# A norm turn after a seven-product matmul stage, taken by halves of the tokens

## What is computed

```python
        f = (jax.nn.gelu(gate, approximate=True) * val) @ w_down[l]     # 2816 -> 1024
        h = h + rms_norm(f, ln_ffn_post[l])
    ...
        h = rms_norm_2(x, norm1[l])                                     # second block, x is h above
        proj = h @ w_in[l]
```

## Time and profile before

| | |
|---|---|
| median of 3 runs | 2959.04 us (2957.28 to 2969.57) |
| the profiled execution | 2959.0 us, span 2957.2 us |
| TensorE matmul busy | 2835.6 us, 96% |
| VectorE, ACT, GpSimd busy | 62%, 43%, 21% |
| mean granted TensorE clock | 0.989 |

### The profile page before, as it was taken

How to read it: one execution, slowest core, us unless ns; L and a number is a source line. 1 busy time by engine, 2 the same in 40 slices (tenths; PEclk the granted TensorE clock), 3 DMA queues, 4 the chain that set the end, 5 groups by cost and what they waited for, 6 DMA issues and landing times.

```text
span 2957.2 us, 47458 instructions
## 1 busy us (share of the span) xinstructions
PE 2835.6 (96%) x19678; PEld 2274.4 (77%) x19678; DVE 1848.0 (62%) x2351; ACT 1269.7 (43%) x1879; POOL 623.0 (21%) x313
## 2 busy tenths in 40 slices
PE   8999998889899999999899999999899999999999
PEld 6877777777688888788678867766578888888887
DVE  3157778852599999866685554565645766653446
ACT  4145555542554555443543433343433423333334
POOL 4310122221100000254151200000012122245443
PEclk9999999999999999999999999999899999999999
DMA  6443330002423333465544553435544344465664
GB/s 216 151 121 114 110 131 30 27 26 79 143 89 106 102 101 107 155 220 180 175 133 153 164 178 122 129 112 160 192 150 131 115 150 145 150 216 196 211 238 171
DMA packets 306280, 413.79 MB, mean 140 GB/s; under 512 B 13569, under 2 KB 189834, under 8 KB 306066
## 3 DMA queue, kind: packets, MB, share of 16 engines
q1 hardware_dynamic: 291090, 363.56, 38.6%
q10 hardware_dynamic: 14976, 47.19, 4.2%
HBM read 280.64 MB, written 130.06 MB: 139 GB/s over the span
## 4 chain that ended last, share of the span: by engine, by line
PE 80%; DVE 8%; DMA 4%; issue 3%; ACT 3%; SPq 1%; POOL 1%; DVEq 0%; ACTq 0%; POOLq 0%
PE ps L511 17%; PE ps L2767 16%; PE ps L3300 13%; PE ps L3082 10%; PE ps L2124 5%; PE ps L695 4%; PE ps L1544 4%; PE ps L2175 2%; PE ps L2194 2%; DVE cb L3385 2%; PE ps L2152 1%; PE ps L1607 1%; PE ps L2155 1%; DMA kl<-qk_lo 1%; DMA residual<-src 1%
## 5 line engine op out<-in xcount | busy, mean ns | idle before, releaser
L477 POOL TENSOR_TENSOR wl<-wraw,wh 128x1024 fp32r<-128x1024 f32 x62 | 157.4, 2538 | 1103.0 <-ACT wh L472 1093.4
L511 PE MATMUL ps<-xh,wh 128*128 128x512 f32 x752 | 237.9, 398 | 5.2 <-POOL wl L477 2.3
L511 PE MATMUL ps<-xl,wh 128*128 128x512 f32 x752 | 233.3, 392 | 0.0
L511 PE MATMUL ps<-xh,wl 128*128 128x512 f32 x752 | 232.9, 391 | 0.0
L472 ACT ACTIVATE wh<-wraw 128x1024 fp32r<-128x1024 f32 x78 | 82.4, 1056 | 266.0 <-PE ps L511 205.3
L2756 POOL TENSOR_TENSOR h_dl<-h_dr,h_dh 128x1024 fp32r<-128x1024 f32 x36 | 94.7, 2633 | 477.8 <-ACT h_dh L2738 477.6
L511 PEld LDWEIGHTS ps<-xh,wh 128*128 128x128 f32 x752 | 139.6, 189 | 46.7 <-issue 9.0
L2767 PE MATMUL ps<-h_dh,h_fh 128*128 128x512 f32 x448 | 174.8, 390 | 0.7 <-POOL h_dl L2756 0.7
L2767 PE MATMUL ps<-h_dh,h_fl 128*128 128x512 f32 x448 | 174.4, 389 | 0.0
L2767 PE MATMUL ps<-h_dl,h_fh 128*128 128x512 f32 x448 | 174.3, 389 | 0.0
L511 PEld LDWEIGHTS ps<-xl,wh 128*128 128x128 f32 x752 | 142.4, 189 | 30.3
(11 more groups left out here) (507 smaller groups left out, 7634.6 us busy)
## 6 DMA issues: line engine op xcount, KB each, us to landing
h_fr<-act_d SPq DMA_DIRECT2D x60, 512.0 KB, 3.9
act_d<-act SPq DMA_DIRECT2D x16, 1792.0 KB, 6.7
wraw<-in_w_in SPq DMA_DIRECT2D x48, 512.0 KB, 5.0
h_dr<-in_w_down SPq DMA_DIRECT2D x44, 512.0 KB, 4.8
r_raw<-in_w_up SPq DMA_DIRECT2D x38, 512.0 KB, 3.9
residual<-src ACTq DMA_DIRECT2D x32, 512.0 KB, 5.1
w_raw<-in_w_up SPq DMA_DIRECT2D x32, 512.0 KB, 5.1
l_fr<-act_d SPq DMA_DIRECT2D x31, 512.0 KB, 3.9
```

The costliest lines, as they stand in the source:

```text
L477: nc.gpsimd.tensor_tensor(wl[:, s, :, :], wraw[:, s, :, :], wh[:, s, :, :].bitcast(F32), ALU.subtract).then_inc(w_lo, 1)
L511: mm = nc.tensor.matmul(ps[:, bank + h, :], w, x[:, h * HALF:(h + 1) * HALF], start=start and k == 0, stop=stop and k == 2)
```

## The change

The turn is made by halves of the tokens. The second half of `f` is complete after P7, so its norm, the new residual and `xh`, `xl` of the second half are made while P4 is multiplied; after P4 the first half follows, while TensorE multiplies the second half by the first two units. Sums of a half (`half_sums`) are made on four column strips of 128 tokens each; squares of the new second-half rows go to `sq1`, which is the memory of `xl`'s first halves. Residuals move in half tiles of 256 KB. Since `xh`'s and `xl`'s second halves are written during P4, P4's steps get homes elsewhere (`last`): three new ones, and a fourth in the first-half parts of `xh` for step 39, so that the loads of steps 36 to 38 wait only for a few sums. Between P4's steps ACT and VectorE take rows of the second half. Beside that, step 2's cast and low part are moved up by one tap pass.

The core of the diff:

```diff
+        def half_sums(of, start, stop, bank, to):
+            for j in range(4):
+                mm = nc.tensor.matmul(ps[QUARTERS[j], bank, to], ones[:, :], of[:, j * EIGHTH:(j + 1) * EIGHTH],
+                                      start=start, stop=stop)
...
+        def second_half_squares_act(act, m):
+            if m < 4:
+                act.wait_ge(down_added, down_added_by(down1, "P3", m))
+            else:
+                act.wait_ge(down_added, down_added_by(down1, "P7", m - 4))
...
+        def second_half_row_dve(dve, kt):
+            s = kt % 2
+            if kt == 0:
+                h1_pe.wait(dve, "spread", 0)
+            h1_dve.done(nc.vector.tensor_tensor(y[:, kt, SECOND], y[:, kt, SECOND], ps[:, 7, :], ALU.mult), f"m{kt}")
+            h1_dve.wait(dve, f"m{kt}", 0)
+            if kt >= 2:
+                h1_dve.wait(dve, f"l{kt - 2}", 0)
+                h1_act.wait(dve, f"s{kt - 2}", 0)
+            dve.wait_ge(h_loaded[s], 16 * (4 + kt // 2 + 1))
+            dve.wait_ge(src_stored[s], 16 * ((16 + kt) // 2))
+            h1_dve.done(nc.vector.scalar_tensor_tensor(
+                out=src[:, s, SECOND], in0=y[:, kt, SECOND], scalar=col("ln_ffn_post", kt), in1=hres[:, s, SECOND],
...
+        def second_half_act(act, kt):
+            tile = src[:, kt % 2, SECOND]
+            h1_dve.wait(act, f"r{kt}", 0)
+            h1_act.done(nc.scalar.activation(xh[:, kt, SECOND], tile, ACT.Identity, scale=col("norm1_2", kt)), f"x{kt}")
+            nc.scalar.activation(y[:, kt, SECOND], tile, ACT.Identity, scale=col("norm1_2", kt))
+            h1_act.done(nc.scalar.activation(sq1[:, kt, FIRST], tile, ACT.Square), f"s{kt}")
+            act.dma_start(residual[kt][:, SECOND], tile).then_inc(src_stored[kt % 2], 16)
...
         def down_load(sp, d, i):
-            if i >= 8 or (i >= 4 and not d.later):
+            if name == "P4" and d.last:
+                if c < 3:
+                    sp.wait_ge(loaded, down_loaded_by(d, i - 4))
+                    sp.wait_ge(down_done, down_done_by(d, d.steps.index(("P6", len(d.kts) - 1))))
+                    sp.wait_ge(g_sum, down_sums_by(d, d.steps.index(("P7", (0, 0, 4)[c]))))
+                else:
+                    sp.wait_ge(down_done, down_done_by(d, i - 4))
+            elif i >= 8 or (i >= 4 and not d.later):
                 sp.wait_ge(down_done, down_done_by(d, i - 4))
...
             for i in range(8, len(down1.steps)):
+                if i == LAST1 + 3:
+                    for kt in (0, 1):
+                        second_half_loads(sp, kt)
+                elif i == LAST1 + 5:
+                    second_half_loads(sp, 2)
                 down_load(sp, down1, i)
...
             ff1_tap(act, FF_TILES - 1, "g")
+            down_hi_act(act, down1, 2)
             ff1_tap(act, FF_TILES - 1, "v")
-            down_hi_act(act, down1, 2)
             ff1_gelu(act, FF_TILES - 1)
...
+            second_half_root_act(act)
+            down_hi_act(act, down1, LAST1 + 3)
+            for kt in (0, 1, 2):
+                second_half_act(act, kt)
+            down_hi_act(act, down1, LAST1 + 4)
+            for kt in (3, 4):
+                second_half_act(act, kt)
+            down_hi_act(act, down1, LAST1 + 5)
+            second_half_act(act, 5)
+            first_half_squares_act(act, 4)
...
-            post_sums_pe(pe, 24, KT - 2)
-            spread_pe(pe, 3)
-            paced_units(pe, U_FA, 0, 16, 32, 4)
+            second_half_products(pe, 0, 1, {
+                2: lambda pe: first_half_sums_pe(pe, 24), 3: lambda pe: second_half_square_sums(pe, range(0, 4)),
+                5: first_half_spread_pe, 7: lambda pe: second_half_square_sums(pe, range(4, KT))})
+            second_half_products(pe, 1, 3, {})
+            first_half_units(pe)
...
                 for x in "gv":
                     ff1_taps(dve, t, x)
-                    if not more and x == "v":
+                    if not more and x == "g":
                         down_lo_dve(dve, down1, 2)
```

More of the change, by code:

```diff
@@ L130 @@
     kept2: list
+    last: list
 CHUNK = 64
+EIGHTH = T // 8
 @dataclass
@@ L568, in spread_pe, with spread_half_pe @@
             mm.then_inc(spread_done, 1)
+        def spread_half_pe(of, half, row):
+            rows = ROWS[row]
+            for w, j in ((spread_even, 2 * row), (spread_odd, 2 * row + 1)):
+                mm = nc.tensor.matmul(ps[:, 6 + half, j * EIGHTH:(j + 1) * EIGHTH], w[rows, :], of[rows, :],
+                                      start=True, stop=True)
+            return mm
         def rstd_copy_act(act, k):
@@ new lines, in second_half_sum_dve, with second_half_sums_pe @@
+        def second_half_sum_dve(dve, m):
+            h1_act.wait(dve, f"q{m}", 0)
+            if m == 0:
+                dve.wait_ge(stat_root, 3)
+                ins = nc.vector.tensor_copy(ss[:, SECOND], sq[:, 0, SECOND])
+            else:
+                h1_dve.wait(dve, f"a{m - 1}", 0)
+                ins = nc.vector.tensor_tensor(ss[:, SECOND], ss[:, SECOND], sq[:, m % 2, SECOND], ALU.add)
+            h1_dve.done(ins, f"a{m}")
+        def second_half_sums_pe(pe):
+            pe.wait_ge(down_added, down_added_by(down1, "P3"))
+            h1_dve.wait(pe, f"a{KT - 1}", 0)
+            h1_pe.done(half_sums(ss[:, SECOND], True, True, STAT_BANK, FIRST_COLS), "sum")
@@ new lines, in second_half_root_act, with second_half_reciprocal_dve, second_half_spread_pe @@
+        def second_half_root_act(act):
+            h1_pe.wait(act, "sum", 0)
+            h1_act.done(nc.scalar.activation(root1[:, :], ps[:, STAT_BANK, FIRST_COLS], ACT.Sqrt,
+                                             bias=small[:, 0:1], scale=1.0 / D), "root")
+        def second_half_reciprocal_dve(dve):
+            h1_act.wait(dve, "root", 0)
+            h1_dve.done(nc.vector.reciprocal(root1[:, :], root1[:, :]), "rec")
+        def second_half_spread_pe(pe):
+            h1_dve.wait(pe, "rec", 0)
+            h1_pe.done(spread_half_pe(root1, 1, 0), "spread0")
+            h1_pe.wait(pe, "spread0", 0)
+            h1_pe.done(spread_half_pe(root1, 1, 1), "spread")
@@ new lines, in second_half_square_sums, with second_half_products @@
+        def second_half_square_sums(pe, kts):
+            for kt in kts:
+                h1_act.wait(pe, f"s{kt}", 0)
+                mm = half_sums(sq1[:, kt, FIRST], kt == 0, kt == KT - 1, STAT_BANK, SECOND_COLS)
+            h1_pe.done(mm, f"p{kts[-1]}")
+        def second_half_products(pe, u, bank, after):
+            for kt in range(KT):
+                h1_dve.wait(pe, f"l{kt}", 0)
+                if kt == 0:
+                    pe.wait_ge(w_lo, U_FA + u + 1)
+                    pe.wait_ge(evac_done, U_FA + u - 1)
+                    pe.wait_ge(down_added, down_added_by(down1, "P4", bank))
+                half_tile(bank, u, kt, SECOND)
+                if kt in after:
+                    after[kt](pe)
```

281 lines of the change are left out of this document (201 added, 80 removed).

## The result

Over 20 runs each the changed kernel took 2965.36 us (median; 2957.05 to 2970.67) and the kernel before 2957.66. The ratio is 1.0024 with a 95% interval of [1.0016, 1.0032]: about 7 us slower. That is under the 0.5% that I had called measurable for this kernel, but clear of zero: with 20 runs the interval is 0.1% to either side. The forecast was 4.5 us faster, and 2965.4 lies 1.4 us above its range. The profiled execution of the change took 2961.96 us (span 2960.2), 3.4 us under its median.

What follows compares the result with a forecast made beforehand. TensorE was taken as the bound, with VectorE pacing the norm turn. 2959.0 us less 2.4 (start of the down stage) less 2.1 (third unit's start, after the loss before the last products) gave 2954.5 us; range 2944 to 2964.

Steps and rivals of the forecast that it cites:

- part 4: First half, after the last products up to the third unit: that unit starts at 1486.2 against 1488.26, -2.1 us.
- part 1: Start of the down stage: one 5.28 us wait becomes 0.9 and 4.1 us; -2.4 us, ends 0 and -4.
- part 3: Second half beside the seventh product: TensorE waits 8.1 us before the last products, the clock falls; 11.8 us lost.
- lower end: Start of the down stage: if the 4.1 us wait costs the clock again, 2.8 is given back, gain 0.
- part 2: Loads of the seventh product's operand steps, the first three issued early: nobody waits for them, cost 0.
- Without the cold clock: Case for the start of the third unit if the clock stays up: -5.7 us in place of -2.1.
- third rival: Adds from row 2 on, both halves: the residual's round trip becomes the bound, 2964.6 us; chance 0.20.
- first rival: Half-width adds beside GpSimd's splits: engines do not take turns, wait 3.7 us, clock stays, 2946 us; chance 0.17.
- second rival: Before the last products: operands arrive in time, no wait, third unit -12.2 us, 2942.8 us; chance 0.08.
- deciding point: Residual's round trip in both halves: it decides once a half tile lands later than 3.3 us.

Runs made afterwards that it cites:

- e5: The changed kernel run again without any edit: ratio to the kernel before 1.0020 [1.0008, 1.0031].
- e3: The change, with casts and low parts of the seventh product's last two operand steps ahead of most second-half rows: ratio to before 1.0005.
- e2: The kernel before with only the change's start part (step 2's cast and low part ahead of the value half's taps): ratio to before 1.0003.
- e8: e7, with TensorE summing squares of the first half's first two rows between the second half's products: ratio to before 1.0020.
- e9: e7, with VectorE's copies out of the last product's banks one row later each, so row 5 comes first: ratio to before 0.9998.
- e10: e9, with TensorE summing squares of the first half's first two rows between the second half's products: ratio to before 0.9994.
- e7: e3, with VectorE's copies out of the last product's banks, and ACT's squares of them, ahead of rows 5 to 7: ratio to before 1.0016.
- e4: The change, with VectorE's T1 moved behind the eviction of fa: ratio to before 1.0024.
- e1: The change, with its start part (step 2's cast and low part moved up) put back as before: ratio to before 1.0019.
- e6: The change, with step 37's cast and low part ahead of half squares and sums, and P7's adds between the square sums: ratio to before 1.0030.
- e12: The kernel before run again without any edit: ratio to before 1.0007 [0.9997, 1.0017].
- e13: The change, with fa's bank copied out raw and multiplied with the reciprocal root later: ratio to before 1.0020.
- e16: The change, with the cast and low part of step 41, the last operand step, one row later: ratio to before 1.0037.

## Why the prediction was wrong

The sign was wrong: +6 to +7 us where I had -4.5. The loss that I took as the largest came as forecast. The gains that were to outweigh it came out too small: the first half and the way to the third unit (part 4) by 6.1 us, the start (part 1), as far as times can tell, by all of its 2.4.

**Cost, part 3, held.** From the first seventh product to the first of the last products I had 30.8 us (from 1413.35, where it begins before) and the traces 31.3 and 30.8; up to the end of the last product 11.0, measured 10.1. TensorE waited 7.0 us where I had 8.1, since it came 1.8 us later than I had it (1437.8 for 1436.0), by the start wait, and by sums and spreads in halves. The rows came within 1.1 us of the list: 1436.8 for the split of step 40 was 1437.8, step 41's 1444.1 was 1444.65. Some luck is in the sum: the last products began 0.7 us later than I had them, but only 8 matmuls there ran at the 1.2 GHz level (12 in e5), where I had 14, which more than made up for it. e3 shows that the wait costs about the time it seems to.

**Cost, part 4, failed, in two terms above all.** Up to the first half's spread I had 7.3 us, measured 7.8. "Then 0.7, eight rows of 2.1, the last low part, and 0.7 of waits for residuals: 19.1" took 21.3 (1462.64 to 1483.97): the third row's square waited 1.98 us for a buffer that TensorE frees only once it has gone through the second half's products. The third row's store left later by that, and the fifth row, which needs the same buffer, waited 0.98 us for it. And "unit 0 ends 1.1 later ... the third unit's weights are then cast and split" took 8.1 us where I had 4.7. I read in the earlier trace rows that the third unit waited for wl and took the split as the only thing there, at 2.5 us, where in the trace of before it took 3.87 beside T1. That trace already needed 7.3 us from the last low part to the unit, so 4.7 was too little before any change. The chain from the last row over squares, root, reciprocal (1.75), spread, copy (1.03) and eviction (1.20) stood hidden behind it by 0.4 us (in the trace of before the eviction ends at 1487.84, the unit starts at 1488.26), and the change lengthened it: the last spread takes 16 short products and 2.3 us, where it was 8 and 1.1. From the seventh product to the third unit, -2.1 became +3.6 in the first pair of traces; the traces of the change have 78.5 and 78.1 us there, those of before 74.9 and 73.5.

**Cost, part 1, failed.** The two waits came nearly as worked out. "TensorE waits 0.9 us and stays warm" held, but that step 3's wait would leave the clock up did not: 0.50 in 1246 to 1248, and step 3, 24 products, took 8.1 us (1244.87 to 1252.99) instead of 5.4. This was the lower end that I gave, 0, and it is what e2 shows. My -2.4 was also taken from a trace of before with 14 cold matmuls; with the 7 of the second trace TensorE starts step 7 41.9 us after the first down product, and the two traces of the change have 42.1 and 42.6. Nor would a clock that stays have saved the gain: e8 has one, and starts step 7 at 44.1, behind a split that ends at 43.9, where I had 41.2 (1264.8). An end below nothing, by waits at steps 7 and 14, I did not give.

**Cost, part 2.** The loads cost nothing that the traces show.

**Slips in the sums.** Without the cold clock part 4 is -2.1 - 2.8 = -4.9, not -5.7, and the third rival's 2964.6 lies outside the range that was to take it in.

**The rivals.** The engines do take turns at every half-width add that met a split, so the first rival is out. The Trainium skill (SBUF — State Buffer, SBUF: two separate sides) has them exclude each other for a whole instruction; the trace agrees, 0.75 us alone and up to 2.17 beside a split, with the end 0.55 us behind the split's. The second rival, operands in time, was out for this order and was what e9 built. I had priced it at -12.2 us to the third unit; e9 and e10 gave 70.0 and 69.0 us there, 4 to 6 under the kernel before: the same missing chain, and TensorE's own new work. The third rival had the right side and the wrong mechanism. Half tiles of the residual landed 3.5 (load) and 3.8 us (store) after issue in this stretch (medians of 14 and 16), longer than the 2.6 to 2.9 I took and over my own deciding point of 3.3:

```profile
residual<-src ACTq DMA_DIRECT2D x16, 256.0 KB, 3.8
hres<-residual SPq DMA_DIRECT2D x14, 256.0 KB, 3.5
```

Yet VectorE waited only 2.9 us for them in all 16 rows (1.6 in the second half, 1.3 in the first). The deciding point was set too low: the first row's store is issued at 1464.16, and the third row's add, which needs that buffer, starts at 1467.85 without a wait, 3.7 us later. The Trainium skill (DMA: Bandwidth & Descriptors, Anatomy of one DMA) gives about 2.0 us plus the bytes at 436 GB/s, and that for transfers that GpSimd issues. By this, an estimate, 256 KB take 2.6 us and not the 3.0 that I had put down; the 3.5 and 3.8 measured here, on SP's and ACT's queues, are longer than both.

**What stays open.** The traces of the change and of before differ by 4.2 us between the marks (pairs), or 5.8 if the 1.7 of the start part's average is laid on the 4.1 of the turn; the times say 5.9 and 7.1. Why the wait at the start of the seventh product is 0.3 to 2.1 us in the changed kernels, and why the splits of step 14 fall beside VectorE's operations in some executions only, was not found.

## What to carry to other kernels

When a stage is cut in halves so that one half hides behind other work, look at who is queued behind the hidden half: here operands behind rows cost more than the half hid, and the cure was an order, not less work. A wait that the profile names is the last of several; before a forecast takes what is behind it as gained, walk every other chain that ends at the same instruction, for one may stand half a microsecond behind. Moving an instruction ahead on one engine can make a loop in which two engines wait for each other in turn as easily as it breaks one (e7), so follow both engines through it once.

## What the runs showed of the chip

- TensorE's clock fell to the 1.2 GHz level behind waits far shorter than the 5.28 us of before: behind 1.84 us in e4 and 1.99 us in e10 (step 14), and behind 1.85 us in e1 and 2.12 us in e6 (start of the seventh product). Behind 1.72 us (e2, step 7) it did not, and once it did not behind 3.41 us (e8, step 3), where 11 other traces fell behind the same wait. In e1, e6 and e10 the products behind it took some 1.6 us more (8 of them at 0.43 us where they take 0.23). Behind the one long wait at the start of the down stage 7 to 14 products were slow, in traces of the same order: before 14, e12 7.
- A half-width add on VectorE that met a split on GpSimd ended 0.55 us behind the split's end, in all 21 cases of seven traces (the change, e3, e4, e5, e9, e13, e16), however long it then lasted (1.05 to 2.49 us; 0.75 alone).
- A product of 128 columns costs almost what one of 256 does. The last spread had 8 products of 256 columns in 1.1 us before (1484.39 to 1485.45) and has 16 of 128 columns in 2.3 us now: 0.13 and 0.14 us each. The half sums and spreads that the change puts into the seventh product are 1.8 of the 2.2 us by which "to last" grows even without a wait (29.8 to 32.0). The Trainium skill (TensorE: Matmul & The Clock Gate, Back-to-back issue gap) says that in a stream of weight loads and matmuls both set the spacing; the trace agrees as far as half the columns did not give half the time.
- A split on GpSimd (2.34 to 2.5 us alone) took 5.09 us beside T1 (2048 columns) on VectorE in e13, and T1 4.37 us in the change, 2.26 in e13. Which of the two pays is not told by the recorded starts: in the change the split starts 0.1 us ahead of T1 and T1 pays, in e13 it starts 0.6 us ahead and pays itself.
